# Sixteen expert teams on one core: gathering tokens and adding expert rows as products of high and low fp32r parts, and choosing tokens for two teams at once

## What is computed

```python
def hierarchical_moe(h, ...):                    # h: [1, 256, 1024]
    ...
    e_val, e_loc = lax.top_k(e_in, TOP_K)        # 2 experts for each token
    e_w = jax.nn.softmax(e_val, axis=-1) * g_w[:, None]
    ...
    def block_ffn(args):                         # per expert, D_EXPERT = 256
        xb = xt[tok]
        hb = jax.nn.silu(xb @ w_gate[e]) * (xb @ w_up[e])
        return (hb @ w_down[e]).astype(F32) * wt[:, None]
    ...
    return jnp.zeros((T, D), F32).at[row_tok].add(yb.reshape(rows, D))
```

## Time and profile before

| | |
|---|---|
| median of 3 runs | 1185.15 us (1185.14 to 1188.02) |
| the profiled execution | 1187.22 us, its span 1185.4 us |
| mean granted clock of TensorE | 0.925 |
| busy share | PE 90%, PEld 75%, DVE 44%, ACT 34%, POOL 13% |
| expert loop (first `gate_up` to end of last `down`) | 847.63 to 1128.82 us |

### The profile page before, as it was taken

One profiled execution on the slowest core, in us unless ns is written; L12 is line 12 of the kernel. 1 busy time (PEld: TensorE's weight loads), 2 busy tenths in 40 slices (PEclk: granted clock), 3 DMA queues, 4 the chain that ended last, 5 costly groups with the idle time before them and its releaser, 6 DMA issues.

```text
span 1185.4 us, 17311 instructions
## 1 busy us (share of the span) xinstructions
PE 1071.2 (90%) x7061; PEld 889.1 (75%) x7062; DVE 521.9 (44%) x944; ACT 404.1 (34%) x682; POOL 152.8 (13%) x216
## 2 busy tenths in 40 slices
PE   3799999989787879999996999879899999999966
PEld 2599999988755869999995999678555646646556
DVE  5545554336632255554336538674232222222254
ACT  3443333433343353334335556633201101101053
POOL 5233331110000123333011000000100000000000
PEclk8799999999766889999998999878899999999988
DMA  6334433436400115453453332048288988988501
GB/s 261 142 107 177 167 143 133 160 122 277 152 1 1 72 71 172 182 190 117 176 216 118 143 112 80 1 170 340 94 356 339 380 336 350 372 339 351 214 1 36
DMA packets 25645, 212.52 MB, mean 179 GB/s; under 512 B 2000, under 2 KB 5344, under 8 KB 5728
## 3 DMA queue, kind: packets, MB, share of 16 engines
q1 hardware_dynamic: 25568, 211.43, 46.2%
HBM read 210.35 MB, written 1.07 MB: 178 GB/s over the span
## 4 chain that ended last, share of the span: by engine, by line
PE 81%; DVE 6%; ACT 5%; issue 3%; POOL 3%; DMA 0%; POOLq 0%; DVEq 0%; ACTq 0%
PE ps L1107 45%; PE ps L1443 9%; PE ps L1428 5%; PE ps L1457 5%; PE ps L1465 4%; PE ps L1098 3%; DVE mix L1564 2%; DVE wl L613 2%; ACT wh L606 2%; POOL sq L479 1%; ACT work L752 1%; PE ps L1201 1%; PE ps L1200 1%; PE ps L1413 1%; PE ps L1144 1%
## 5 line engine op out<-in xcount | busy, mean ns | idle before, releaser
L613 DVE TENSOR_TENSOR wl<-ring,wh 128x2048 fp32r<-128x2048 f32 (+2 forms) x110 | 223.3, 2034 | 225.3 <-ACT wh L606 225.3
L606 ACT ACTIVATE wh<-ring 128x2048 fp32r<-128x2048 f32 (+2 forms) x110 | 187.1, 1705 | 318.6 <-PE ps L1107 314.1
L1107 PE MATMUL ps<-xh,wh 128*128 128x256 f32 (+3 forms) x760 | 218.9, 288 | 8.9 <-DVE xl L2074 7.0
L1107 PE MATMUL ps<-xh,wl 128*128 128x256 f32 (+3 forms) x760 | 216.6, 285 | 0.0
L1107 PE MATMUL ps<-xl,wh 128*128 128x256 f32 (+3 forms) x760 | 216.4, 285 | 0.0
L1107 PEld LDWEIGHTS ps<-xh,wh 128*128 128x128 f32 (+3 forms) x760 | 143.2, 188 | 10.9 <-issue 9.2
L1107 PEld LDWEIGHTS ps<-xh,wl 128*128 128x128 f32 (+3 forms) x760 | 143.2, 188 | 0.2
L1107 PEld LDWEIGHTS ps<-xl,wh 128*128 128x128 f32 (+3 forms) x760 | 143.1, 188 | 0.0
L1443 PE MATMUL ps<-wring,xb 128*64 128x512 f32 x512 | 112.7, 592 | 2.3 <-issue 2.3
L1107 PE MATMUL ps<-acth,wh 128*128 128x272 f32 (+1 forms) x352 | 102.6, 292 | 3.8 <-POOL actl L494 3.8
L1107 PE MATMUL ps<-acth,wl 128*128 128x272 f32 (+1 forms) x352 | 101.4, 288 | 0.0
(11 more groups left out here) (334 smaller groups left out, 1618.5 us busy)
## 6 DMA issues: line engine op xcount, KB each, us to landing
wring<-in_w_eg SPq DMA_DIRECT2D x32, 2048.0 KB, 10.4
ring<-in_w_gu SPq DMA_DIRECT2D x22, 2048.0 KB, 7.9
wring<-in_w_ed SPq DMA_DIRECT2D x16, 2048.0 KB, 8.3
ring<-in_w_dn SPq DMA_DIRECT2D x16, 1408.0 KB, 5.9
ring<-in_w_z SPq DMA_DIRECT2D x7, 2048.0 KB, 7.8
ring<-in_w_out SPq DMA_DIRECT2D x4, 1152.0 KB, 5.1
ring<-in_w_q SPq DMA_DIRECT2D x2, 2048.0 KB, 14.0
ring<-in_w_o SPq DMA_DIRECT2D x2, 2048.0 KB, 10.5
```

The source lines that it names most:

```text
L606: act.activation(wh[:, j, 0:size], ring[:, slot, j * size:(j + 1) * size], ACT.Copy)\
L613: dve.tensor_tensor(wl[:, j, 0:size], ring[:, slot, j * size:(j + 1) * size], wh[:, j, 0:size].bitcast(F32), ALU.subtract).then_inc(sem("l ...
L1107: ins = mm(o, p, q, start=first and n == 0, stop=last and n == 2)
```

## The change

- `gather`: `h2` becomes two fp32r tiles. ACT writes the high part `h2h`, DVE the rest `h2l` (four new DVE operations inside `routing`), and each product is h2h x psel + h2l x psel, with `psel` now fp32r. `psel` has 256 columns, for two teams. A call `gather(n)` makes half of the 1024 rows for both teams of a pair, so there is still one call for each team, now 16 fp32r matmuls of 256 columns; it is done two teams ahead instead of one. Two calls stand ahead of the loop, and the last two teams have none. `xb` has two buffers of two teams each.
- `combine`: the row weights move out. `he` is scaled with the slot's weight (`small[:, 178:179]`, the sum of a row of the old `comb`, from an accumulator output in `weigh`), and `combine` adds rows by a matrix `places` of zeros and ones. The rows `y` are split: ACT copies both banks to `yh`, DVE subtracts into `yl` (L2114 of the changed kernel), 16 fp32r matmuls in place of 8 fp32 ones.
- On DVE `select` runs once for two teams, twice as wide; `placed(b)` is new: `weigh` for the next team and a comparison that writes `places`.

```diff
-            def gather(select, made):
+            def pick(out, c, select):
+                at = slice(c * P, (c + 1) * P)
+                for k in range(NB):
+                    mm(out, h2h[:, k, at], select[:, k, :], start=(k == 0), stop=False)
+                    ins = mm(out, h2l[:, k, at], select[:, k, :], start=False, stop=(k == NB - 1))
+                return ins
+            def gather(n):
                 for half in range(2):
-                    for c in range(4):
-                        for k in range(NB):
-                            at = slice((half * 4 + c) * P, (half * 4 + c + 1) * P)
-                            ins = mm(ps[:, 5 + half, c * P:(c + 1) * P], h2[:, k, at], select[:, k, :],
-                                     start=(k == 0), stop=(k == NB - 1))
-                    ins.then_inc(sem(made), 1)
+                    for i in range(2):
+                        ins = pick(ps[:, 5 + half, i * 2 * P:(i + 1) * 2 * P], n % 2 * 4 + half * 2 + i, psel[n // 2 % 2])
+                    ins.then_inc(sem("gathered"), 1)
...
-            gather(psel[0], "gathered")
+            gather(0)
+            for evacuated in ("xb_ready", "xb_ready_d"):
+                pe.wait_ge(sem(evacuated), 1)
+            gather(1)
...
-                if b + 1 < TEAMS:
-                    pe.wait_ge(sem("psel_ready"), b + 2)
+                if b + 2 < TEAMS:
+                    pe.wait_ge(sem("psel_ready"), b // 2 + 2)
                     if b:
-                        pe.wait_ge(sem("y_ready"), b)
-                    gather(psel[(b + 1) % 2], "gathered")
+                        pe.wait_ge(sem("y_low"), 2 * b - 1)
+                    for evacuated in ("xb_ready", "xb_ready_d"):
+                        pe.wait_ge(sem(evacuated), b + 2)
+                    gather(b + 2)
...
+            for q in range(4):
+                dve.wait_ge(sem("h2h_ready"), q + 1)
+                part = slice(q % 2 * 512, (q % 2 + 1) * 512)
+                dve.tensor_tensor(h2l[:, q // 2, part], ps[:, 1 + q, :], h2h[:, q // 2, part].bitcast(F32), ALU.subtract)\
+                   .then_inc(sem("h2l_ready"), 1)
...
+            def placed(b):
+                if b >= 2:
+                    dve.wait_ge(sem("chunk_used"), b * CHUNKS)
+                chain(weigh(dve, chain, weighed, 176, 178))
+                dve.tensor_scalar(places[b % 2][:, :], weighed, 0.0, None, ALU.is_gt).then_inc(sem("places_ready"), 1)
...
             for b in range(TEAMS):
                 extra(b)
                 dve.wait_ge(sem("sg_ready"), b + 1)
-                dve.tensor_tensor(he, sgate, ps[:, 4, FE:2 * FE], ALU.mult).then_inc(sem("he_ready"), 1)
+                dve.scalar_tensor_tensor(he, ps[:, 4, FE:2 * FE], small[:, 178:179], sgate, ALU.mult, ALU.mult)\
+                   .then_inc(sem("he_ready"), 1)
+                if b + 2 < TEAMS:
+                    gathered(b + 2)
+                for i in range(2):
+                    dve.wait_ge(sem("y_ready"), 2 * b + i + 1)
+                    dve.tensor_tensor(yl[:, i * 512:(i + 1) * 512], ps[:, 6 + i, :], yh[:, i * 512:(i + 1) * 512].bitcast(F32),
+                                      ALU.subtract).then_inc(sem("y_low"), 1)
                 if b + 1 < TEAMS:
-                    gathered(b + 1)
-                weigh(dve, chain, comb[b % 2], 176).then_inc(sem("comb_ready"), 1)
...
-                dve.tensor_copy(ysb[b % 2][:, 512:D], ps[:, 7, :]).then_inc(sem("y_ready_d"), 1)
-                if b + 2 < TEAMS:
-                    selected(b + 2)
+                    dve.wait_ge(sem("he_ready"), b + 1)
+                    placed(b + 1)
+                if b % 2 and b + 3 < TEAMS:
+                    selected(b // 2 + 2)
```

More of the change, by code:

```diff
@@ L179, in bass_two_blocks @@
         with ExitStack() as turn:
-            h2 = sb("h2", [P, NB, D], F32, turn)
-            xb = [sb(f"xb{i}", [P, KD, P], F32, turn) for i in range(2)]
+            h2h = sb("h2h", [P, NB, D], F32R, turn)
+            h2l = sb("h2l", [P, NB, D], F32R, turn)
         ctx.enter_context(nc.sbuf_tensor("x_room", [P, 18 * SEQ], F32))
@@ L186, in bass_two_blocks @@
             actl = sb("actl", [P, NF, T], F32R, turn)
+        with ExitStack() as turn:
+            yh = sb("yh", [P, D], F32R, turn)
+            yl = sb("yl", [P, D], F32R, turn)
+            places = [sb(f"places{i}", [P, SEQ], F32R, turn) for i in range(2)]
+            psel = [sb(f"psel{i}", [P, NB, 2 * P], F32R, turn) for i in range(2)]
+            pselx = sb("pselx", [P, NB, P], F32R, turn)
+            moe_room = 2 * D + 2 * SEQ + 4 * NB * P + NB * P
         work = sb("work", [P, 2 * NF * T])
@@ L239, in bass_two_blocks @@
         take = carve()
+        take(moe_room)
         wproj = take(2560)
         ppT = take(KD, SEQ)
-        ysb = [take(D) for _ in range(2)]
-        comb = [take(SEQ) for _ in range(3)]
-        psel = [take(NB, P) for _ in range(3)]
+        combx = take(SEQ)
         spread = take(4, SEQ)
@@ L249, in bass_two_blocks @@
         rscr = take(700)
-        second = take(SEQ)
+        weighed = take(SEQ)
         spare = take(SEQ)
@@ L517, in _ @@
             pool.memset(brow[0:NH, :], NEG).then_inc(sem("brow_ready"), 1)
[L518 to L524, removed]
+            whole = mix[:, 0:2, :].rearrange("p a b -> p (a b)").bitcast(I32)
+            pool.iota(whole[:, 0:2 * P], pattern=[[ROUNDS * P, 2], [1, P]], base=0, channel_multiplier=0)
+            first = 2 * P
+            pool.iota(whole[:, first:first + NE], pattern=[[ROUNDS * P, TEAMS], [FEW, TEAM]], base=0, channel_multiplier=0)
+            first += NE
+            pool.iota(whole[:, first:first + ROUNDS - 1], pattern=[[FEW, ROUNDS - 1]], base=FEW, channel_multiplier=0)
+            first += ROUNDS - 1
+            chain(pool.iota(whole[:, first:first + 1], pattern=[[0, 1]], base=0, channel_multiplier=1))
+            pool.tensor_copy(iota[:, :], whole[:, 0:2 * P]).then_inc(sem("iota_ready"), 1)
+            pool.tensor_copy(ranks[:, :], whole[:, 2 * P:2 * P + NE + ROUNDS]).then_inc(sem("iota_ready"), 1)
             pool.wait_ge(sem("consts_loaded"), 32)
@@ L1460, in down, with combine @@
                 return ins
-            def combine(y, weights, last=False):
+            def combine(parts, weights, last=False):
                 for c in range(KD):
-                    ins = mm(ps[:, c // 2, c % 2 * SEQ:(c % 2 + 1) * SEQ], y[:, c * P:(c + 1) * P], weights,
-                             start=False, stop=last, skip_group_check=True)
+                    for y in parts:
+                        ins = mm(ps[:, c // 2, c % 2 * SEQ:(c % 2 + 1) * SEQ], y[:, c * P:(c + 1) * P], weights,
+                                 start=False, stop=last and y is parts[-1], skip_group_check=True)
                     if last:
@@ L1482, in extra @@
                         over.wait("dve", "select")
-                        gather(psel[2], "over_pe")
+                        gather_extra()
                         over.wait("act", "xb")
@@ L1697, in routing @@
             chain(dve.scalar_tensor_tensor(small[:, 168:172], base, float(P - FEW), rank, ALU.mult, ALU.add))
-            select(dve, chain, psel[0], 168).then_inc(sem("psel_ready"), 1)
+            select(dve, chain, psel[0], 168, iota[:, :]).then_inc(sem("psel_ready"), 1)
             dve.tensor_copy(at, small[:, 168:172]).then_inc(sem("columns_ready"), 1)
```

107 lines of the change are left out of this document (61 added, 46 removed).

## The result

The changed kernel takes 1155.74 us (1154.71 to 1163.07, 4 runs) against 1185.25 before (4 runs too); the ratio on record is 0.9739, 95% interval [0.971, 0.9767] (the two medians alone give 0.975). It is faster, as forecast, but 17.7 us slower than the 1138 of the forecast and above its range. The profiled execution took 1156.66 us with a span of 1154.9.

The account below looks back on a forecast made before the run. TensorE's own work was taken to bound the loop: −51.3 us in the loop, +3.3 ahead, +0.6 after, sum −47.4, so 1139.8 us profiled and 1138 us median. The 80% range was 1132 to 1152 us.

Parts of the forecast that it names:

- TensorE's own work paced the loop: Loop: TensorE's matmuls set the 17.89 us a team, with the loads the next limit, close behind.
- 1.93 us each: Gather and combine in the loop: 16 fp32r products each at 0.120 us, against 3.77 and 3.46 us before.
- as counted: VectorE's list in a team: `he` ends near 7.9 us after `down` at worst, hidden by gather until 8.8.
- where I allowed 0.15: Weighing on VectorE: the accumulator read as a second instruction adds some 0.15 us, held by the margin before `he`.
- Nothing waits: Expert loads in the loop: team 15's first chunk lands at 207 us, TensorE asks for it at 216.
- the 397 that I worked out as needed: Expert loads in the loop: no cost down to 83.9 MB in 211 us, 397 GB/s.
- I take no wait in teams 1 to 13: Middle teams of the loop: no TensorE wait for `he`; bounds nothing and 1 us in each.
- 14.52: Middle team of the loop, thirteen of them: 14.52 us in place of 17.89.
- +3.3: Ahead of the loop: later first gather, half clock and a second gather add 3.3 us, between +2 and +6.
- +0.6: After the loop: ScalarE copies two banks instead of one before its table load and weight splitting, 0.6 us more.
- Clock loss after an idle stretch: Rival, loop: `he` 2 us late each team brings half clock, 5 us a team lost, 1203 us; 3 in 100.
- The loads pace the loop: Rival, loop: at 353 GB/s the 40th chunk lands 25 us after it is wanted, 1163 us; 10 in 100.

Follow-up runs that it names:

- experiment 1: Changed kernel without the rounds for crowded experts on TensorE (no register load, branch or skipped code there): 1143.29 us, ratio 0.9595 to the kernel before.
- experiment 4: Kernel before the change with one more unused load of 1.05 MB a team in teams 2 to 15: 1190.65 us, ratio 0.9982.
- experiment 3: Changed kernel with every expert chunk from team 2 on loaded only to a half, all code kept: 1146.34 us, ratio 0.9614 to the kernel before.
- experiment 5: Changed kernel unaltered, run once more on another chip: 1163.42 us, ratio 0.9804 to the kernel before.
- experiment 7: Changed kernel with the skipped rounds for crowded experts written twice on TensorE: 1212.74 us, ratio 1.0234 to the kernel before.
- experiment 2: Changed kernel with TensorE's register load and branch kept but only the semaphore increment in the taken side: 1143.38 us, ratio 0.9602 to the kernel before.
- experiment 8: Kernel before the change with the skipped rounds written twice on TensorE: 1210.71 us, ratio 1.0178 to the kernel before unaltered.

## Why the prediction failed

**What held.** TensorE's own work paced the loop. A 128x128 by 256-column fp32r product costs 0.12 us there as in the earlier trace rows; gather takes 2.11 us and combine 1.91 in the chain (885.28 to 887.39 and 887.61 to 889.52), against 1.93 each. VectorE is in time with `he` even behind the selection: it ends 7.9 us after the end of `down` in team 6, as counted, with silu and not VectorE's list as what came last. The accumulator read is a row of its own, as the Trainium skill has it (VectorE: DVE Perf Modes, section "Two Vector instructions with no wait between them"), and takes 0.08 us where I allowed 0.15:

```profile
962.38 0.43 DVE L1763 SCALAR_TENSOR_TENSOR work<-work 128x256 f32<-128x256 f32 x1
962.73 0.08 DVE L1763 DVE_READ_ACCUMULATOR work<-work 128x1 f32 x1
```

The loads: "Nothing waits" was right. They ran at 414 GB/s for 205 us in experiment 1, against the 397 that I worked out as needed (216 − 3.5 = 212.5 us in hand would make it 395). The Trainium skill's limit of about 358 GB/s for a core (DMA: Bandwidth & Descriptors, section "Where 436 GB/s comes from") does not hold for this core by that number.

**The step that failed.** "So TensorE's own work paces the loop, and the loads are the next limit", and with it "I take no wait in teams 1 to 13". Between the two stood a third limit that I did not list: TensorE's program. I treated the load's share of the DMA engines as a matter for the loads alone. The signs were there: the row of instruction packets on the page of the kernel before, and in the kernel a jump over a second copy of the team in each team. The change shortened the team by 3.2 us, brought the DMA engines from 0.88 to about 1.00, and left the code to pass nearly as long (1.6 and 1.4 packets a team). Full engines at 17.9 us a team give no wait (experiment 4); 14.7 us a team beside half loads gives 4.2 us of waits (experiment 3); both together give 11.7. So the pace was needed, it did about a third by itself, and the full engines did the rest.

**The account.** The sum was 1139.8 us for a profiled execution, the measured one 1156.7. The five waits are 11.7 us; the `gate_up` behind them is longer by 1.69 + 1.91 at the half clock and 3 x 0.22 otherwise, 4.3 us: 15.9 together. A team is 14.69 and not 14.52, as each fp32r stream takes nearly 0.1 us to get going (the first product of gather starts 0.22 us ahead of the second, that of combine 0.20, the others 0.12), 2.2 us over thirteen teams, and 0.3 in the other three. Two small terms came out better: ahead of the loop +2.4 and not +3.3, mostly since the clock had risen for the second gather (2.1 us and not 2.8) and the first started 2.45 us later and not 2.9, and behind it about 0 and not +0.6. Sum 15.9 + 2.5 − 0.9 − 0.7 = 16.8 of the missing 16.9. (The median is 17.7 off: it lies 0.9 and not 2.1 us below the profiled execution.)

**The rivals.** Clock loss after an idle stretch did occur, but the wait ahead of it was not VectorE's, and it was not as priced. The rival had 3 us lost behind a wait of 2 us; here 1.69 and 1.91 us were lost behind 4.17 and 3.37 (and 2.98 behind 3.84 in experiment 5), and in experiment 7 `gate_up` still took 7.09 us behind waits of 2.38, 2.83 and 3.13. "The loads pace the loop" would have given a stretch late in the loop with the load as releaser; there is none.

**Open.** What starts the fetch of a packet, how far ahead of its use, and why in the changed kernel only teams with an odd number had the waits, and which of them. The trace shows when packets of about 16 KB come and how many, not what is in them. That the packet at a wait holds the code behind the jump is argued from its place and from experiments 2, 7 and 8, not seen.

## What to carry to other kernels

Before pricing a faster loop, ask what else it consumes per turn: code that is skipped is fetched too (0.6, 1.4 and 2.3 packets a team with none, one and two copies of it), through the DMA engines that the loads use. An "issue" wait right behind a branch is a sign of it; look for an instruction packet that ends just before the wait does, and test it by emptying the skipped side and by doubling it. Put the rare case in a second copy of the loop behind the common one, so that nothing is jumped over in the loop, and look at every engine where the long jump then stands.

## What the runs showed of the hardware

- Code that is never executed cost 2 to 4% of the time: with the skipped rounds doubled, the kernel before went from 1189.3 to 1210.7 us and the changed one from 1163.4 to about 1212 us.
- A load stream on one core held 414 GB/s over 205 us, and TensorE beside it stayed busy 203.9 us.
- After idle stretches of 4.17 and 3.37 us the next 6.87 us of matmuls took 8.56 and 8.78; after 1.20 to 1.63 us it took 7.09.
- TensorE resumed 1.7 to 1.8 us after the end of a 16 KB instruction packet in all ten waits of the changed kernel's two profiles; the packet itself took 0.9 to 1.1 us.
